# A two-block model forward pass: the rings of split weights begin 64 bytes behind a line of 2048

## The reference

```python
def swiglu(x, w_in, w_out):                 # five of these: 1024 -> 2 x 2816 -> 1024
    g, u = jnp.split(x @ w_in, 2, axis=-1)
    return (jax.nn.silu(g) * u) @ w_out

h = h + 0.5 * swiglu(rms_norm(h, ffn1_norm[i]), ffn1_w_in[i], ffn1_w_out[i])
h = h + m                                   # m: a mixer between projections x @ w_in, (..) @ w_out
h = h + 0.5 * swiglu(rms_norm(h, ffn2_norm[i]), ffn2_w_in[i], ffn2_w_out[i])
```

## Time and profile before

| what | value |
|---|---|
| median of 3 runs | 2819.62 us (2818.82 to 2820.05) |
| span of the profiled execution | 2817.5 us |
| PE busy | 2790.9 us, 99%, 16386 matmuls |
| PEld busy | 2391.3 us, 85%, 16386 loads |
| DVE / ACT / POOL busy | 59% / 48% / 56% |
| share of PE in the chain that ended last | 94% |
| mean granted clock of TensorE | 0.999 |

### The profile page before, as it was taken

How to read it: one execution, slowest core, us unless ns; L and a number is a source line. 1 busy time by engine, 2 the same in 40 slices (tenths; PEclk the granted TensorE clock), 3 DMA queues, 4 the chain that set the end, 5 groups by cost and what they waited for, 6 DMA issues and landing times.

```text
span 2817.5 us, 45558 instructions
## 1 busy us (share of the span) xinstructions
PE 2790.9 (99%) x16386; PEld 2391.3 (85%) x16386; DVE 1657.6 (59%) x2703; ACT 1346.4 (48%) x2076; POOL 1571.1 (56%) x872
## 2 busy tenths in 40 slices
PE   8999999999999999999999999999999999999999
PEld 6998877899889998888999886665688888799987
DVE  6777147677616774135777416579788464477730
ACT  5554257555425554243555334557444444455531
POOL 6775445677547774444777443158633373367743
PEclk9999999999999999999999999999999999999999
DMA  3234322232332233332223332112222342123332
GB/s 136 105 104 115 103 82 82 91 104 104 111 99 90 104 109 105 100 106 89 91 104 120 101 94 77 53 53 66 71 89 70 103 149 75 53 103 107 109 98 77
DMA packets 80685, 267.91 MB, mean 95 GB/s; under 512 B 11168, under 2 KB 13216, under 8 KB 80560
## 3 DMA queue, kind: packets, MB, share of 16 engines
q1 hardware_dynamic: 77904, 262.01, 28.4%
q10 hardware_dynamic: 2656, 4.26, 0.5%
HBM read 263.09 MB, written 2.10 MB: 94 GB/s over the span
## 4 chain that ended last, share of the span: by engine, by line
PE 94%; DVE 3%; ACT 1%; issue 1%; DMA 0%; POOL 0%; ACTq 0%; SPq 0%; DVEq 0%
PE bank L460 17%; PE bank L462 17%; PE bank L461 17%; PE bank L716 10%; PE bank L718 10%; PE bank L717 10%; PE bank L547 1%; PE bank L548 1%; PE bank L549 1%; PE bank L1635 1%; PE bank L2047 1%; PE bank L2915 1%; PE bank L2647 0%; PE bank L2056 0%; PE bank L2627 0%
## 5 line engine op out<-in xcount | busy, mean ns | idle before, releaser
L448 POOL TENSOR_TENSOR w_lo<-w_stage,w_hi 128x1024 fp32r<-128x1024 f32 (+1 forms) x228 | 535.2, 2353 | 714.0 <-ACT w_hi L424 713.5
L424 ACT ACTIVATE w_hi<-w_stage 128x1024 fp32r<-128x1024 f32 (+1 forms) x412 | 421.0, 1027 | 367.2 <-PE bank L462 303.5
L803 POOL TENSOR_TENSOR w_lo<-w_stage,w_hi 128x1024 fp32r<-128x1024 f32 (+1 forms) x176 | 327.3, 1859 | 202.1 <-ACT w_hi L424 202.1
L460 PE MATMUL bank<-xg_hi,w_hi 128*128 128x512 f32 x976 | 396.2, 406 | 5.0 <-DVE h_raw L1063 3.8
L461 PE MATMUL bank<-xg_lo,w_hi 128*128 128x512 f32 x976 | 381.2, 391 | 0.0
L462 PE MATMUL bank<-xg_hi,w_lo 128*128 128x512 f32 x976 | 381.2, 391 | 0.0
L455 POOL TENSOR_TENSOR w_lo<-w_stage,w_hi 128x1024 fp32r<-128x1024 f32 (+1 forms) x96 | 234.9, 2453 | 261.7 <-ACT w_hi L424 217.3
L460 PE MATMUL bank<-h_hi,w_hi 128*128 128x512 f32 x880 | 342.3, 389 | 0.0
L461 PE MATMUL bank<-h_lo,w_hi 128*128 128x512 f32 x880 | 342.3, 389 | 0.0
L462 PE MATMUL bank<-h_hi,w_lo 128*128 128x512 f32 x880 | 342.3, 389 | 0.0
L718 PE MATMUL bank<-xg_hi,w_lo 128*128 128x256 f32 x1056 | 299.2, 283 | 0.0
(11 more groups left out here) (530 smaller groups left out, 6599.0 us busy)
## 6 DMA issues: line engine op xcount, KB each, us to landing
w_stage<-w_up SPq DMA_DIRECT2D x220, 512.0 KB, 4.2
w_stage<-w_down SPq DMA_DIRECT2D x80, 512.0 KB, 3.5
w_stage<-merge SPq DMA_DIRECT2D x36, 512.0 KB, 3.4
w_stage<-w_down SPq DMA_DIRECT2D x40, 384.0 KB, 3.2
w_stage<-hg_qfg SPq DMA_DIRECT2D x12, 512.0 KB, 3.4
w_stage<-rec_r SPq DMA_DIRECT2D x8, 512.0 KB, 3.5
w_stage<-rec_y SPq DMA_DIRECT2D x8, 512.0 KB, 3.4
w_stage<-rec_out SPq DMA_DIRECT2D x8, 512.0 KB, 3.4
```

Of the source, the lines that this page charges most:

```text
L424: act.activation(w_hi[:, r, 0:w], w_stage[:, r, 0:w], ACT.Copy).then_inc(w_hi_ready, 1)
L448: pool.tensor_tensor(w_lo[:, r, 0:w], w_stage[:, r, 0:w], f32(w_hi[:, r, 0:w]), ALU.subtract).then_inc(w_lo_ready, 1)
L460: pe.matmul(out, w_hi[:, r, c], hi, start=start, stop=False)
L803: pool.tensor_tensor(w_lo[:, r, cs], w_stage[:, r, cs], f32(w_hi[:, r, cs]), ALU.subtract).then_inc(w_lo_ready, 1)
```

## The change

It moves tiles and alters no instruction otherwise. `w_hi` and `w_lo` begin 64 bytes behind a line; what lies behind them is on lines again, 2048 bytes further on with respect to the tiles ahead. `s1_w` and `s2_w` begin 192 and 320 bytes behind a multiple of 1024, which is 64 bytes behind a multiple of 128. `s3_w`, `xsum`, `xg_hi`, `xg_lo`, `h_hi`, `h_lo` and the other moving tiles keep their place relative to a line. The unused scratch shrinks from 16384 to 1024 bytes, which makes room, and all tiles begin further down.

```diff
     LINE = 2048
+    WEIGHTS_BEHIND_LINE = 64
...
     w_stage = place("w_stage", [P, RING, UNIT])
+    cursor[0] += WEIGHTS_BEHIND_LINE
     w_hi = place("w_hi", [P, RING, UNIT], F32R)
     w_lo = place("w_lo", [P, RING, UNIT], F32R)
+    cursor[0] += LINE - WEIGHTS_BEHIND_LINE
...
-    s1_w = place("s1_w", [P, 2, T], F32R, at=work + 33 * KB)
-    s2_w = place("s2_w", [P, 2, T], F32R, at=work + 37 * KB)
+    s1_w = place("s1_w", [P, 2, T], F32R, at=work + 32 * KB + 128 + WEIGHTS_BEHIND_LINE)
+    s2_w = place("s2_w", [P, 2, T], F32R, at=work + 36 * KB + 256 + WEIGHTS_BEHIND_LINE)
...
-    nc = bacc.Bacc("TRN2", target_bir_lowering=False, num_devices=1)
+    nc = bacc.Bacc("TRN2", target_bir_lowering=False, num_devices=1, dynamic_dma_scratch_size=1024)
```

## The result

The changed kernel takes 2838.78 us (median of 3 runs, 2837.97 to 2839.27), the kernel before 2819.62. The ratio on record is 1.0063, with a 95% interval of 1.0043 to 1.0083; the two medians by themselves give 1.0068, which lies inside it. It is slower, by over three times what a measurement of this kernel can tell from no change. The forecast was 16 us faster. The profiled spans differ alike: 2837.5 against 2817.5 us.

A forecast was written before the change was run, and what follows sets the result against it. PE was taken to bound the kernel, through the distance between matmul starts. Terms -22.1, -1.1 and +7.0 us gave -16.2 us: span 2801.3 us, median 2803.4 us, range 2755 to 2848 us.

The forecast's parts named there:

- The mechanism: On PE, moving-row reads and the next stationary load hinder each other, depending on how far apart they start.
- The second rival: Only the moving row's place counts, so only 480 pairs with moving weights gain: -1.1 us, 2818.5 us; chance 0.15.
- the rule weighed against mine: Skill page: loading next weights takes no read bandwidth from the running matmul, so the stationary operand's place can't matter.
- The 6672 pairs: 512-column rows on a line with weight slices stationary, 2224 per line: each priced to gain 2.2 ns.
- The third rival: Slower: the offset's sign matters, as the moving stream must pass the slice on 10032 pairs; slower had chance 0.25.
- its hard end: Passing costs 4.4 ns on each of 10032 pairs, 44.1 us; with other terms 50.0 us slower, 2869.6 us.
- Its milder end: Passing costs as much as it saves, so the 7.0 us loss on `xsum` stands alone: 5.9 us slower, 2825.5 us.
- 3360 pairs of 256 columns: `xg` (1056 per line) and `mem` (64 per line) with the slice moved 64 bytes: each to gain 2.2 ns.
- the first rival: Same cause, but pairs fall into the quick rhythm, gaining 6.8 ns each: 64.5 us faster, 2755 us; chance 0.22.
- 480 pairs with weights moving: Weights as moving operand get the arrangement of `xsum` exactly: 2.2 ns each, 1.1 us gained.
- `xsum` with `s1_w`, `s2_w`, `w_hi`, `w_lo`: 3168 up-projection pairs lose their 64-byte distance and go from 117.8 back to 120.0 ns: 7.0 us lost.
- the likeliest case: The small rhythm, 2.2 ns per pair: 16.2 us faster, median 2803.4 us, own range 2795 to 2812; chance 0.33.

The follow-up runs named there:

- e1_places: Bare runs of 48 matmuls without the model, row and slice moved by 0 to 448 bytes; 512 columns: 226.7 ns on the line, 233.3 with the slice 64 ahead.
- e12_ring_256: Kernel before with only the weight rings moved, by 256 bytes in place of 64, and the smaller scratch: 2820.19 us, ratio 1.0000.
- e5_fine: Bare matmul runs without the model: slice offsets in 16-byte steps, then slices of 64 and 32 columns; 512 columns on the line: 230.0 and 231.7 ns.
- e11_wide_only: Against the kernel before, only units of the plain products and token layers 64 bytes behind; step units and sums as before: 2858.66 us, ratio 1.0136.
- e3_scratch_only: Kernel before with only the smaller scratch and 2048 bytes of room behind the rings: 2820.34 us, ratio 0.9998.

## Why the prediction was wrong

**What bounds the kernel** was right: PE for 94% of the chain before and after, the other engines' busy time within 2.9 us of what it was. The `h` pairs, which have no pause before or after, alone account for 17.6 us.

**The mechanism** was right in its outer form. The place of the stationary operand counts, and with slices of 128 columns it counts as a distance to the moving row. `e1_places` shows it by moving both, and `e12_ring_256` in the kernel. That the two streams hinder each other is not shown; the narrow slices of `e5_fine` speak against its simplest form. The second rival is dead, and with it the reading of the rule weighed against mine. By the Trainium skill, TensorE: Matmul & The Clock Gate, section "Part 2: What happens when you issue a matmul", two independent read ports keep the weight load out of the matmul's way; the measurement decides here, and 226.7 against 233.3 ns for a shift of the slice alone is not what that sentence leads one to expect.

**The step that failed** is this one: "as the loss with both on a line is 13.3 ns for 256 and for 512 columns alike, I use the same 2.2 ns". An equal loss with both on a line says nothing about what a shift does. With 512 columns the shift costs 6.7 ns where I booked a gain of 2.2. The 6672 pairs, booked at -14.7 us of the -22.1, measured +38.7 us (with the 48 that the prediction's rows lack): 53 us of error in one term. `e11_wide_only` has this term nearly by itself, and is 38.4 us slower than the kernel before. The third rival had the direction and the cause in its heading, that the sign matters, and priced its hard end at 4.4 ns on all 10032 pairs; but the reason that it gave, one stream passing the other, is not supported: with 256 columns the same sign wins. Its milder end, 5.9 us slower, took the shift to be worth nothing, which is wrong for both forms.

**The other terms**, by their sizes:
- 3360 pairs of 256 columns: booked at -7.4 us, measured -20.5. The quick rhythm of the earlier trace rows, which I held to need a halt, runs in the steady steps: 113.3 ns. This is the first rival, nearly true for a third of the pairs: 6.1 ns each, where it had 6.8.
- 480 pairs with weights moving: booked at -1.1 us, measured +2.0. They have the arrangement of `xsum`, but with 512 columns, and the row 64 ahead costs 2.5 ns there by `e1_places`. In the kernel their distances without pauses went from 228.0 to 229.4 ns, which is 0.7 us of the 2.0; the rest is in pauses.
- `xsum` with `s1_w`, `s2_w`, `w_hi`, `w_lo`: booked at 120.0 ns and +7.0 us. Over all 88 steps `s2_w` was at 119.9 ns and the others at 119.2, and as `s1_w` had been at 118.3 and not at 117.8, this cost 4.9 us. Nearly all of it came back within the step: `s3_w`, which I left at 117.8 ns, fell to 113.3, 4.6 us, so that all `xsum` pairs together measured +0.3 us. That these two cancel was in no part of the sum.
- The other engines and the smaller scratch, booked at nothing: `e3_scratch_only` found nothing.

With the measured terms the sum is 38.7 - 20.5 + 2.0 + 0.3 - 0.4 = +20.1 us, against +20.0 of span. The range was wide enough to hold the time, since it took in part of the third rival; the likeliest case was of the wrong sign, and that the time fell inside is no merit of the sum.

**What the rows of before could have told:** The earlier trace rows have one arrangement for 512 columns and two for 256, so two thirds of the sum stood on a form of which the trace has no second point. The prediction said so in its last sentence and still gave a faster kernel 0.58.

What stays open: why the distance modulo 256 bytes counts at all; why a narrower slice on the line makes 512 columns slower and, at 64 columns, 256 columns faster; and what selects 113.3 or 117.8 ns with 256 columns.

## What to carry to other kernels

A price per instruction holds for the form on which it was read. When a change moves several forms at once, look for a row for each; a form that the trace shows in one arrangement only gets a range of both signs, and if it holds most of the count, so does the whole forecast. And where a mixed change shifts the time little, sum the start-to-start distances by class before judging it: here +41 and -21 us lay behind +20, and keeping only the good half made the kernel 0.63% faster than before (0.49% to 0.77%).

## What the runs showed of the hardware

- With a slice of 128 columns and rows of 512, the time from one matmul's start to the next depends on how far the stationary slice begins ahead of the moving row, modulo 256 bytes: 226.7 ns at 0 and 256, 233.3 at 64 and 233.1 at 320, and 229.0 at 192 against 229.2 with the row 64 bytes ahead, which is the same distance modulo 256.
- With 256 columns an offset that is bad with 512 is the good one: 120.0 ns on the line, 113.3 or 117.8 with the slice 64 bytes ahead.
- In the whole kernel, moving the slices of the plain products and token layers by 64 bytes cost 38.4 us of 2820, and moving all the weight rings by 256 bytes cost nothing (ratio 1.0000, 0.9990 to 1.0010).
- A narrower slice is no remedy with rows of 512 columns: 230.0 ns with 64 columns and 231.7 with 32, against 226.7 with 128, all on the line. With rows of 256 columns it can be: 113.4 ns with 64 columns on the line, against 120.0 with 128.
- Rows of 256 columns have rhythms that outlast the cause. Steps with the same addresses took 9.57 and 9.86 us in turns, and untouched `xg` pairs moved between 114.0 and 117.8 ns when only the matmuls ahead of them were placed elsewhere.
